# Four buffers in place of two for the inputs of a chunked scan, each loaded two tiles ahead

## The chip, the cores and the metric

The kernel runs on one core of one Trainium2 chip. The time is the device time of one execution in microseconds (us), and less is better. TensorE is called PE here, VectorE DVE, ScalarE ACT, GpSimd POOL and SyncE SP; SP computes nothing and issues most of the DMA transfers.

## What is computed

One layer of a diffusion backbone: a combined input projection, four mixers side by side, and an output projection. The change lies in the stage that runs two of the mixers together, neighbourhood attention (A) and gated linear attention (D). Cut to these two:

```python
# A: each query sees an 8x16 window of keys around it, and 512 context keys
s_lat = einsum('bhrqd,bhrikd->bhrqik', qg, kg) + bias
s_ctx = einsum('bhrqd,bhcd->bhrqc', qg, ck)
p = softmax(concatenate([s_lat, s_ctx], -1))
o = einsum('bhrqik,bhrikd->bhrqd', p_lat, vg) + einsum('bhrqc,bhcd->bhrqd', p_ctx, cv)

# D: a scan over chunks of 64 tokens, forward and backward
att = where(causal, einsum('bhntk,bhnsk->bhnts', q_dec, k_inv), 0)
o_intra = einsum('bhnts,bhnsv->bhntv', att, vc)
upd = einsum('bhnsk,bhnsv->bhnkv', k_end, vc)
def step(state, inp):
    d_c, u_c = inp
    return d_c[..., None] * state + u_c, state
o_inter = einsum('bhntk,bhnkv->bhntv', q_dec, s_start)
```

## The kernel before

The stages follow one another: modulation, two projection stages, this attention and scan stage, a Fourier stage, the output stage. Between stages all engines meet at a barrier.

The stage `attention_scan_stage` walks over 34 tiles of 128 tokens. A tile `i` of the grid is a block of 8 rows (`jb`, `b`) and one of four column strips (`c`, 0 to 3), so four tiles make a block; tiles 32 and 33 are the prompt. In the same step a tile does attention for its 128 queries, head by head (`h`, 0 to 3), and two chunks of the scan in each direction. Tiles 0 to 7 and 24 to 33 are written out, tiles 8 to 23 run in a loop over pairs of blocks.

Each engine has its own list of instructions, written by hand and tied together by semaphores. What matters here:

- **SP**, at the start of tile `i`, waits until PE is done with all of tile `i-1` (`pv_done`, `od_mm`). Then it issues, in this order: the values of tile `i+1` (`load_values`, four DMAs into `v_win`), the scan's inputs of tile `i+1` (`load_scan`, two DMAs into `scan` and two into `kv`), and one part of the next block's input: the queries at `c` = 0 (`q_hi`, `q_lo`), the keys' high part at `c` = 1 (`k_hi`), their low part at `c` = 2 (`k_lo`). After that it waits for the tile's output and stores it. All these DMAs go through one queue, SP's.
- **PE** does for each head `turn` (transposes of the probabilities, L1265 for the window and L1273 for the context), `scores` for later heads (L1244), and `values` (L1301). At `h` = 0 the last matmuls of `values` wait for the scan's inputs (`t_in`), after which `scan_scores` uses them (L1310). At `h` = 1 of the strip `c` = 3, the transposes of L1273 wait for the next block's keys (`k_in`), since the scores that follow need them.
- **POOL** reorders the queries of tile `i+1` (`order_queries`, L1118, semaphore `q_set`) and keeps the running state (`keep_state`, L1135, L1139). Ahead of the first tile it orders tile 0's queries, then waits for the initial state `s_at` (`st_in`); only then does it order tile 1's queries, for which PE waits at L1273 of tile 0, head 1.

Ahead of the tiles SP issues the masks' biases for the first strip, the values and the scan's inputs of tile 0, then `s_at`, then the other biases:

```python
            load_bias(0, BLOCKS - 1)
            load_values(0, BLOCKS - 1, 0)
            load_scan(0, 0)
            for d in DIRS:
                sp.dma_start(s_at[here(d), :]...).then_inc(st_in, 16)
```

Of the kernel before, what the change touches and what calls it, by code (L numbers as in the profile page):

```python
# [24 lines left out]
P = 128  # L25
# [8 lines left out]
W_GRP = 256  # L34
# [841 lines left out]
def attention_scan_stage(nc, io, keep, early):  # L876
# [15 lines left out]
    DIRS = range(2)  # L892
# [6 lines left out]
    with stage(nc) as (ctx, new_sem):  # L899
# [20 lines left out]
        max_c, max_w, neg_m, total, r_total = (sb(n, [P, 2]) for n in ("max_c", "max_w", "neg_m", "total", "r_total"))  # L920
        sums = sb("sums", [P, 2, 2])
        ones = sb("ones", [P, NH, P])
        scan = two("scan", [P, 3 * 512 + 8])
        kv = [two(f"kv{d}_", [P, 2, 2 * W_GRP]) for d in DIRS]
        mask = sb("mask", [P, C])
        s_at, s_mid, s_dec = (sb(n, [P, W_GRP]) for n in ("s_at", "s_mid", "s_dec"))
        od_sb = two("od_sb", [P, 2, W_GRP])
# [18 lines left out]
             "q_set", "s_done", "maxc_done", "w_done", "max_done", "exp_done", "sum_done", "rsum_done", "t_done", "t0_sb", "t1_sb", "pv_done", "o_done",  # L946
             "att_mm", "att_sb", "upd_mm", "mid_set", "mid_done", "new_set", "new_done", "kept", "od_mm", "od_done", "st_out"))
        bias_in = [sem(f"bias_in{e}") for e in range(3)]
        k_in, q_in, v_in, t_in, o_sent, od_sent = ([sem(f"{n}{s}") for s in range(2)] for n in ("k_in", "q_in", "v_in", "t_in", "o_sent", "od_sent"))
        block = ctx.enter_context(nc.Block())  # L950

        def tile_of(d, i):
# [31 lines left out]
        def _(sp):  # L984
# [44 lines left out]
            load_bias(0, BLOCKS - 1)  # L1029
            load_values(0, BLOCKS - 1, 0)  # L1030
            load_scan(0, 0)
            for d in DIRS:
                sp.dma_start(s_at[here(d), :].rearrange("k (h v) -> k h v", h=NH), io["state_gla"][0, 0, d].rearrange("h k v -> k h v")).then_inc(st_in, 16)
            for e in range(1, 3):
# [3 lines left out]
            for tile in query_tiles(sp):  # L1038
                i, jb, b, c, kb = tile
                nxt = next_tile(*tile)  # L1040
                if not isinstance(i, int):
                    ni, nb = nxt[0], nxt[2]
                    ahead(sp, 4 * i, 4 * i + 5, b * (BQ * W_GRP * 4), *((key_at(nb) + 4 * m) * (GRID_W * P1_W * 4) for m in range(4)),
                          *(n for d in DIRS for n in (tile_of(d, ni) * (HD * SCAN_W * 4), tile_of(d, ni) * (P * 2 * W_GRP * 4), tile_of(d, i - 1) * (P * W_GRP * 4))))
                    if c == 0:
                        ahead(sp, jb * 16, jb * 8, (b + 1) * (BQ * 4))
                    elif c < 3:
                        ahead(sp, key_at(b + 1) * (GRID_W * 4))
                if nxt:
                    if not isinstance(i, int) or i:  # L1050
                        sp.wait_ge(pv_done, 4 * i)
                        sp.wait_ge(od_mm, i)
                    load_values(nxt[0], nxt[2], nxt[3])
                    load_scan(nxt[0], nxt[3] % 2)
                if c < 3 and b is not None:
                    after = next_tile(i + 3 - c, jb, b, 3, kb)
                    if c == 0:
                        if not isinstance(jb, int) or jb:
                            sp.wait_ge(s_done, jb * 16)
                            sp.wait_ge(q_set, jb * 8)  # L1060
                        load_queries(after[1], after[2], after[4])
                    else:
                        load_keys(after[1], after[2], after[4], c - 1)
                if isinstance(jb, int) and jb < 2 and c in (0, 2, 3):
                    e = (0, None, 1, 2)[c]
                    sp.wait_ge(bias_clear, 3 + 3 * jb + e + 1)
                    load_bias(e, jb)
                sp.wait_ge(o_done, 4 * i + 5)
                if b is None:
                    sp.dma_start(io["ya"][i * P:(i + 1) * P, :], o_sb[c % 2][:, :]).then_inc(o_sent[c % 2], 16)  # L1070
                else:
                    sp.dma_start(io["ya"][bass.ds(b * BQ, BQ), :].rearrange("(r x) n -> r x n", x=GRID_W)[:, c * QB_C:(c + 1) * QB_C, :],
                                 o_sb[c % 2][:, :]).then_inc(o_sent[c % 2], 16)
                if not isinstance(i, int) or i:
                    sp.wait_ge(od_done, i)
                    for d in DIRS:
                        sp.dma_start(io["od"][d, bass.ds(tile_of(d, i - 1) * P, P), :], od_sb[1 - c % 2][:, d, :]).then_inc(od_sent[1 - c % 2], 16)
# [12 lines left out]
        def _(pool):  # L1090
# [33 lines left out]
            def keep_state(i, s, n):  # L1124
                state = s_mid if n else s_at
                if n:
                    pool.wait_ge(mid_done, i + 1)
                else:
                    pool.wait_ge(new_done, i + 1)
                    pool.wait_ge(t_in[s], (i - s) * 32 + 64)  # L1130
                    if not isinstance(i, int) or i > 1:
                        pool.wait_ge(od_mm, i - 1)
                for d in DIRS:
                    c = n if d == 0 else 1 - n
                    pool.tensor_tensor(kv[d][s][here(d), c, W_GRP:], state[here(d), :], ones[here(d), 0:2, :].rearrange("k a b -> k (a b)"), ALU.mult).then_inc(kept, 1)  # L1135
                pool.wait_ge(kept, 4 * i + 2 * n + 2)
                if not (n and isinstance(i, int) and i == GRID_T - 1):
                    heads = lambda a: a.rearrange("k (p h v) -> k p h v", p=2, h=2)
                    pool.tensor_tensor(heads(s_dec[:, :]), heads(state[:, :]), chunk_dec[s][:, :, :, n].unsqueeze(3).broadcast_to([P, 2, 2, HD]),  # L1139
                                       ALU.mult).then_inc(new_set if n else mid_set, 1)  # L1140
                else:
                    pool.sem_inc(new_set, 1)
# [4 lines left out]
            for tile in query_tiles(pool):  # L1147
                i, jb, b, c, kb = tile
                nxt = next_tile(*tile)
                if nxt:  # L1150
                    order_queries(*nxt)
                keep_state(i, c % 2, 0)
                if isinstance(jb, int) and jb < 2 and c in (0, 2, 3):
                    pool.wait_ge(max_done, 4 * i + 4)
                    e = (0, None, 1, 2)[c]
                    clear_bias(e)
                    pool.wait_ge(bias_clear, 3 + 3 * jb + e + 1)
                keep_state(i, c % 2, 1)

        @block.scalar  # L1160
        def _(act):
# [65 lines left out]
        def _(pe):  # L1227
# [48 lines left out]
            def values(tile, h):  # L1276
# [15 lines left out]
                for n, (m, val) in enumerate(todo):  # L1292
                    if n == len(todo) - 1:
                        if h == 0:
                            pe.wait_ge(t_in[s], (i - s) * 32 + 64)
                            if not isinstance(i, int) or i:
                                pe.wait_ge(od_done, i)
                        elif h == 1:
                            pe.wait_ge(att_sb, 2 * i + 2)
# [44 lines left out]
            for tile in query_tiles(pe):  # L1344
                i, jb, b, c, kb = tile
                for h in range(NH):
# [1 line left out]
                    scores(units_ahead(tile, h, 3), units_ahead(tile, h, 2))  # L1348
                    values(tile, h)
                    if h == 0:  # L1350
                        scan_scores(i, c % 2)
                    elif h == 1:
                        scan_updates(i, c % 2)
                    elif h == 3:
                        scan_out(i, c % 2)

        @block.vector
        def _(dve):
# [47 lines left out]
            for tile in query_tiles(dve):  # L1406
                i, jb, b, c, kb = tile
                for h in range(NH):
# [9 lines left out]
                    cols = N_PROMPT if b is None else WIN_P  # L1418
                    dve.tensor_copy(p_t[p][:, 0:cols], ps_t[0][:, 0:cols]).then_inc(t0_sb, 1)  # L1419
                    if h == 1:  # L1420
                        mask_scores(i, c % 2)
                    elif h == 2:
                        first_update(i)
                    elif h == 3:
# [448 lines left out]
```

## Time and profile before

| | us |
|---|---|
| median of 3 runs | 2808.14 (2800.19 to 2809.13) |
| the profiled execution | 2806.83 |
| its span, first to last instruction | 2805.1 |
| the stage's 34 tiles, from PE's first matmul of the stage to its last scan output | 1642.5 to 2223.7 |
| PE busy over the whole span | 2565.9 (91%) |
| PE busy from 1660 to 2224 | 527.7 of 564 |

The rows of the next section are of three kinds. In the **timeline** a row is a run of like instructions on one engine: start and length in us, engine, source line, what it writes and reads, the shape and how many; in brackets the time for which the engine stood idle before it, and what ended that. In the **waits** a row says which engine and line waited for what: us in total, how many times, the longest. In the **windows** a row is a stretch of time: its length, the busy time of PE, PE's weight loads, DVE, ACT and POOL with the number of instructions, the clock that PE was granted (1.00 is 2.4 GHz, 0.50 is 1.2 GHz), the mean busy share of the core's 16 DMA engines, and the GB/s that they moved. A share a little over 1 comes from packets that overlap on an engine. A row of the **DMA issues** gives how many, their size, and the median time from issue to landing, where it is known.

### The profile page before, as it was taken

How to read it: one execution, taken by the hardware profiler on the slowest of the kernel's cores; microseconds unless marked ns; L12 is line 12 of the kernel's file. 1: busy time of each engine (PE TensorE's matmuls, PEld its weight loads, DVE VectorE, ACT ScalarE, POOL GpSimd, SP SyncE). 2: the span in 40 equal slices, each digit the busy share in tenths (PEclk: the TensorE clock that was granted, in tenths of full speed). 3: DMA queues.
4: the chain of work that ended last, by engine and by line, in shares of the span. 5: the costliest groups of instructions: out<-in, count | busy, mean ns of one | idle time of the engine just before them, and what ended most of it. 6: DMA issues, size and time to landing. Idle time of an engine off the chain costs nothing. (4 is left out here: it accounts for less than half of the span.)

```text
span 2805.1 us, 53370 instructions
## 1 busy us (share of the span) xinstructions
PE 2565.9 (91%) x19036; PEld 2056.4 (73%) x19036; DVE 1271.6 (45%) x2644; ACT 984.1 (35%) x1991; POOL 740.7 (26%) x1145
## 2 busy tenths in 40 slices
PE   3899999999999949999999969998999764999999
PEld 1688888888888838888888857777777522788887
DVE  2444344344343343333333336776777322666555
ACT  2444444444444342222222125565656311111110
POOL 2233333233233210000000024333333201344442
PEclk8999999999999979999999979999999687999999
DMA  7433333333333263222222268877776497766664
GB/s 287 145 103 119 114 111 118 108 115 121 101 120 117 76 215 123 97 97 93 93 93 95 71 133 175 178 172 162 166 164 157 123 289 216 243 210 213 205 202 136
DMA packets 281020, 412.05 MB, mean 147 GB/s; under 512 B 43893, under 2 KB 201365, under 8 KB 277291
## 3 DMA queue, kind: packets, MB, share of 16 engines
q1 hardware_dynamic: 267372, 376.67, 46.6%
q10 hardware_dynamic: 12959, 32.33, 3.2%
q8 instruction: 95, 1.56, 0.3%
q0 software_dynamic: 544, 1.09, 0.2%
q14 instruction: 50, 0.41, 0.1%
HBM read 275.64 MB, written 134.34 MB: 146 GB/s over the span
## 5 line engine op out<-in xcount | busy, mean ns | idle before, releaser
L258 PE MATMUL p_ps_m<-p_w_hi,p_h_hi 128*128 128x512 f32 x1904 | 771.0, 405 | 21.1 <-DVE p_h_lo L779 19.4
L259 PE MATMUL p_ps_m<-p_w_lo,p_h_hi 128*128 128x512 f32 x1904 | 750.7, 394 | 0.0
L260 PE MATMUL p_ps_m<-p_w_hi,p_h_lo 128*128 128x512 f32 x1904 | 749.2, 393 | 0.0
L258 PEld LDWEIGHTS p_ps_m<-p_w_hi,p_h_hi 128*128 128x128 f32 x1904 | 359.3, 189 | 100.3 <-issue 20.2
L260 PEld LDWEIGHTS p_ps_m<-p_w_hi,p_h_lo 128*128 128x128 f32 x1904 | 358.8, 188 | 80.6
L259 PEld LDWEIGHTS p_ps_m<-p_w_lo,p_h_hi 128*128 128x128 f32 x1904 | 359.4, 189 | 72.6
L258 PE MATMUL o_ps_y<-o_w_hi,o_y_hi 128*128 128x512 f32 x544 | 217.4, 400 | 9.8 <-DVE o_y_lo L1773 9.8
L260 PE MATMUL o_ps_y<-o_w_hi,o_y_lo 128*128 128x512 f32 x544 | 217.4, 400 | 0.0
L259 PE MATMUL o_ps_y<-o_w_lo,o_y_hi 128*128 128x512 f32 x544 | 215.6, 396 | 0.0
L770 DVE TENSOR_TENSOR p_xt<-p_xt,p_ps_r 128x1024 f32<-128x1024 f32 x68 | 82.7, 1216 | 193.4 <-PE p_ps_r L679 193.4
L512 POOL TENSOR_TENSOR p_ve<-p_ss,p_eps 128x1 f32<-128x1 f32 x68 | 12.9, 190 | 565.5 <-ACT p_xr L576 565.5
L552 POOL TENSOR_TENSOR p_la<-p_la,p_cum 128x512 f32<-128x512 f32 x34 | 44.0, 1294 | 426.7 <-ACT p_cum L589 426.7
L773 DVE TENSOR_SCALAR p_xt<-p_xt,mod 128x128 f32<-128x128 f32 x544 | 146.1, 344 | 2.5
L1419 DVE COPY a_p_t<-a_ps_t 128x512 f32<-128x512 f32 (+1 forms) x136 | 91.7, 674 | 117.0 <-PE a_ps_t L1265 116.8
L779 DVE TENSOR_TENSOR p_h_lo<-p_xt,p_h_hi 128x1024 fp32r<-128x1024 f32 x68 | 83.3, 1226 | 98.8 <-ACT p_h_hi L581 98.8
L1699 ACT ACTIVATE o_y_hi<-o_ps_t 128x512 fp32r<-128x512 f32 x68 | 36.9, 596 | 258.4 <-PE o_ps_t L1728 258.4
L258 PEld LDWEIGHTS o_ps_y<-o_w_hi,o_y_hi 128*128 128x128 f32 x544 | 102.8, 189 | 33.3 <-issue 10.1
L259 PEld LDWEIGHTS o_ps_y<-o_w_lo,o_y_hi 128*128 128x128 f32 x544 | 102.8, 189 | 25.0
L260 PEld LDWEIGHTS o_ps_y<-o_w_hi,o_y_lo 128*128 128x128 f32 x544 | 102.7, 189 | 23.8
L1301 PEld LDWEIGHTS a_ps_o<-a_v_win,a_p_t 128*64 128x64 f32 x2112 | 75.9, 141 | 54.6 <-issue 39.2
L1370 DVE TENSOR_REDUCE a_max_c<-a_ps_c 128x1 f32<-128x512 f32 x128 | 88.1, 688 | 45.2 <-PE a_ps_c L1244 43.9
L1301 PE MATMUL a_ps_o<-a_cv,a_p_t 128*64 128x64 f32 x2048 | 91.0, 225 | 18.6 <-DMA a_kv<-s_kv 16.5
(216 smaller groups left out, 4541.3 us busy)
## 6 DMA issues: line engine op xcount, KB each, us to landing
p_xr<-in_x_sample SPq DMA_DIRECT2D x64, 512.0 KB, 3.8
p_xt<-in_x_sample_t SPq DMA_DIRECT2D x64, 512.0 KB, 4.5
a_scan<-s_scan SPq DMA_DIRECT2D x68, 258.0 KB, 5.9
s_scan<-p_w_raw SPq DMA_DIRECT2D x136, 128.0 KB, 2.4
a_kv<-s_kv SPq DMA_DIRECT2D x68, 256.0 KB, 6.2
a_v_win<-s_p SPq DMA_DIRECT2D x132, 128.0 KB
o_x<-in_x_sample SPq DMA_DIRECT2D x32, 512.0 KB, 4.5
out_y_sample<-o_y ACTq DMA_DIRECT2D x32, 512.0 KB, 4.4
```

The source lines that it names most:

```text
L258: pe.matmul(out, left_hi(k), right_hi(k), start=(k == 0), stop=False)
L259: pe.matmul(out, left_hi(k), right_lo(k), start=False, stop=False)
L260: last = pe.matmul(out, left_lo(k), right_hi(k), start=False, stop=(k == K8 - 1))
L512: pool.tensor_tensor(ve[s][:, :], ss[s][:, :], eps[:, 0:1], ALU.add).then_inc(ve_done, 1)
L552: pool.tensor_tensor(la[:, :, :], la[:, :, :], cum[:, :, :], ALU.subtract).then_inc(la_done, 1)
L770: dve.tensor_tensor(xt[s][:, :, :], xt[s][:, :, :], ps_r[:, s, :].unsqueeze(1).broadcast_to([P, K8, P]), ALU.mult).then_inc(normed, 1)
L773: last = dve.tensor_scalar(xt[s][:, k, :], xt[s][:, k, :], keep["mod"][:, 1, k, j:j + 1], keep["mod"][:, 0, k, j:j + 1], ALU.mult, ALU.add)
L779: dve.tensor_tensor(h_lo[s][:, :, :], xt[s][:, :, :], h_hi[s][:, :, :], ALU.subtract).then_inc(lo_done, 1)
L1301: last = pe.matmul(ps_o[z * HD:z * HD + HD, at:at + HD], p_t[p][:, m * P + z * HD:m * P + z * HD + HD], val, start=(n == 0), stop=(n == le ...
L1370: dve.tensor_reduce(max_c[:, p:p + 1], ps_c[p][:, :], AX.X, ALU.max).then_inc(maxc_done, 1)
L1419: dve.tensor_copy(p_t[p][:, 0:cols], ps_t[0][:, 0:cols]).then_inc(t0_sb, 1)
L1699: act.activation(y_hi[s][:, 4 * b:4 * b + 4, :], ps_t[b][:, :, :], ACT.Copy).then_inc(hi_done, 1)
```

## The change

Four buffers of `scan` and `kv` stand in place of two, one for each strip `c`, and four semaphores `t_in`. In tile `i` SP issues the scan's inputs of tile `i+2`, at the place where it issued those of `i+1`; ahead of the tiles it issues those of tile 0 and of tile 1. POOL, before it writes the state into `kv`, waits for the scan output of tile `i-4` in place of that of tile `i-2`. PE, DVE and ACT do the same work in the same order. Nothing else moves.

```diff
-        scan = two("scan", [P, 3 * 512 + 8])
-        kv = [two(f"kv{d}_", [P, 2, 2 * W_GRP]) for d in DIRS]
+        scan = [sb(f"scan{c}", [P, 3 * 512 + 8]) for c in range(4)]
+        kv = [[sb(f"kv{d}_{c}", [P, 2, 2 * W_GRP]) for c in range(4)] for d in DIRS]
...
+        t_in = [sem(f"t_in{c}") for c in range(4)]
...
             load_scan(0, 0)
+            load_scan(1, 1)
             for d in DIRS:
                 sp.dma_start(s_at[here(d), :]
...
                     load_values(nxt[0], nxt[2], nxt[3])
-                    load_scan(nxt[0], nxt[3] % 2)
+                    if not (isinstance(i, int) and i + 2 > LAST_STEP):
+                        load_scan(i + 2, (c + 2) % 4 if b is not None else c + 2)
...
-                    pool.wait_ge(t_in[s], (i - s) * 32 + 64)
-                    if not isinstance(i, int) or i > 1:
-                        pool.wait_ge(od_mm, i - 1)
+                    pool.wait_ge(t_in[s], (i - s) * 16 + 64)
+                    if not isinstance(i, int) or i > 3:
+                        pool.wait_ge(od_mm, i - 3)
...
-                            pe.wait_ge(t_in[s], (i - s) * 32 + 64)
+                            pe.wait_ge(t_in[c], (i - c) * 16 + 64)
```

Two places on SP show it. The first is ahead of the tiles: SP's rows from the values of tile 0 to the biases of the second and third strip, before (numbers behind a name are the buffers):

```order
L1007 DMA a_v_win0<-s_p1 128x1x256 x4
L1013 DMA a_scan0<-s_scan 64x1032
L1015 DMA a_kv0_0<-s_kv 64x2x512
L1013 DMA a_scan0<-s_scan 64x1032
L1015 DMA a_kv1_0<-s_kv 64x2x512
L1033 DMA a_s_at<-in_state_gla 64x4x64 x2
L1023 DMA a_bias<-s_btab 16x4x256 x16
```

And now, the same place on SP:

```order
L1008 DMA a_v_win0<-s_p1 128x1x256 x4
L1014 DMA a_scan0<-s_scan 64x1032
L1016 DMA a_kv0_0<-s_kv 64x2x512
L1014 DMA a_scan0<-s_scan 64x1032
L1016 DMA a_kv1_0<-s_kv 64x2x512
L1014 DMA a_scan1<-s_scan 64x1032
L1016 DMA a_kv0_1<-s_kv 64x2x512
L1014 DMA a_scan1<-s_scan 64x1032
L1016 DMA a_kv1_1<-s_kv 64x2x512
L1035 DMA a_s_at<-in_state_gla 64x4x64 x2
L1024 DMA a_bias<-s_btab 16x4x256 x16
```

Four more DMAs, the scan's inputs of tile 1, stand between those of tile 0 and the initial state. The second place is tile 2, the strip `c` = 2 of a block: SP's rows from the scan's inputs to the low part of the keys, before:

```order
L1013 DMA a_scan1<-s_scan 64x1032
L1015 DMA a_kv0_1<-s_kv 64x2x512
L1013 DMA a_scan1<-s_scan 64x1032
L1015 DMA a_kv1_1<-s_kv 64x2x512
L987 DMA a_k_lo1<-s_qk_lo 128x2x960
```

And now:

```order
L1008 DMA a_v_win1<-s_p1 128x1x256 x4
L1014 DMA a_scan0<-s_scan 64x1032
L1016 DMA a_kv0_0<-s_kv 64x2x512
L1014 DMA a_scan0<-s_scan 64x1032
L1016 DMA a_kv1_0<-s_kv 64x2x512
L988 DMA a_k_lo1<-s_qk_lo 128x2x960
```

The number of DMAs, their sizes and their place ahead of `k_lo` are the same; only the tile that they are for is another (tile 4 in place of tile 3).

## Rows read from the trace of the kernel before

**Rows 1.** Window of the stage, from tile 0's second head to the last tile.

```profile
1660.00:2224.00 564.00, 527.73 (x9160) 421.34 (x9159) 386.21 (x1039) 318.13 (x814) 203.48 (x333) 0.97 0.72 162
```

**Rows 2.** Waits of PE in the whole stage, from 1656 to 2226.

```profile
PE a_ps_o L1301 <- DMA a_kv<-s_kv: 16.5, 15, 2.7
```

**Rows 3.** Waits of PE in tiles 12 to 15 (1863 to 1930).

```profile
PE a_ps_o L1301 <- DMA a_kv<-s_kv: 3.3, 3, 1.3
```

**Rows 4.** Waits of PE in tiles 20 to 27 (1999 to 2134).

```profile
PE a_ps_o L1301 <- DMA a_kv<-s_kv: 5.0, 4, 1.8
PE a_ps_t L1273 <- DMA k_lo<-s_qk_lo: 1.0, 1, 1.0
...
PE a_ps_t L1273 <- DMA a_k_lo<-s_qk_lo: 0.6, 1, 0.6
```

**Rows 5.** Timeline of SP in tile 14, strip c = 2.

```profile
1897.33 4.70 SPq L1007 DMA_DIRECT2D a_v_win<-s_p  x4
...
1904.96 0.72 SPq L1015 DMA_DIRECT2D a_kv<-s_kv  x1
1905.78 0.55 SPq L987 DMA_DIRECT2D k_lo<-s_qk_lo  x1
```

**Rows 6.** Timeline of PE in tile 15, heads 0 and 1.

```profile
1916.38 0.34 PE L1301 MATMUL a_ps_o<-a_cv,a_p_t 128*64 128x64 f32 x4 [1.02 <-DMA a_kv<-s_kv]
...
1917.73 0.66 PE L1265 MATMUL a_ps_t<-ident,a_s_sb 128*128 128x128 f32 x4
1918.97 0.66 PE L1273 MATMUL a_ps_t<-ident,a_s_sb 128*128 128x128 f32 x4 [0.58 <-DMA k_lo<-s_qk_lo]
```

**Rows 7.** Windows in and just after tiles 12 to 15.

```profile
1867.00:1881.00 14.00, 13.99 (x240) 11.04 (x238) 10.55 (x27) 8.83 (x23) 4.07 (x8) 1.00 0.86 163
...
1899.00:1904.00 5.00, 4.39 (x82) 3.62 (x82) 2.46 (x6) 2.26 (x6) 2.07 (x3) 1.00 0.28 102
1904.00:1913.00 9.00, 8.99 (x166) 7.34 (x165) 7.24 (x22) 5.77 (x15) 3.75 (x7) 1.00 1.05 225
1916.00:1919.00 3.00, 2.04 (x41) 1.66 (x41) 0.76 (x3) 0.99 (x3) 2.07 (x3) 1.00 0.28 100
1933.00:1935.00 2.00, 1.69 (x14) 1.35 (x14) 1.02 (x3) 0.59 (x2) 0.78 (x2) 1.00 0.08 20
```

**Rows 8.** DMA issues of the stage.

```profile
a_scan<-s_scan SPq DMA_DIRECT2D x68, 258.0 KB, 5.9
a_kv<-s_kv SPq DMA_DIRECT2D x68, 256.0 KB, 6.2
a_v_win<-s_p SPq DMA_DIRECT2D x132, 128.0 KB
```

**Rows 9.** Timeline of SP ahead of the tiles.

```profile
1641.19 1.47 SPq L1013 DMA_DIRECT2D a_scan<-s_scan  x1
...
1644.03 0.61 SPq L1015 DMA_DIRECT2D a_kv<-s_kv  x1
1644.68 1.27 SPq L1033 DMA_DIRECT2D a_s_at<-in_state_gla  x2
```

**Rows 10.** Timeline of POOL at the start: the queries of tile 1.

```profile
1658.15 0.87 POOL L1118 TENSOR_TENSOR a_q_hi_t<-q_hi,a_ones 128x128 fp32r<-128x128 f32 x2 [15.94 <-DMA a_s_at<-in_state_gla]
1658.97 0.87 POOL L1118 TENSOR_TENSOR a_q_lo_t<-q_lo,a_ones 128x128 fp32r<-128x128 f32 x2
```

**Rows 11.** Timeline of PE in tile 0, heads 0 and 1.

```profile
1657.52 0.34 PE L1301 MATMUL a_ps_o<-a_cv,a_p_t 128*64 128x64 f32 x4 [2.70 <-DMA a_kv<-s_kv]
...
1659.02 1.11 PE L1265 MATMUL a_ps_t<-ident,a_s_sb 128*128 128x128 f32 x4
1659.99 1.09 PE L1273 MATMUL a_ps_t<-ident,a_s_sb 128*128 128x128 f32 x4
```

**Rows 12.** Windows at the start of the stage.

```profile
1643.00:1651.00 8.00, 5.54 (x22) 3.48 (x19) 3.60 (x11) 2.10 (x6) 0.00 (x0) 0.50 1.05 194
1651.00:1657.50 6.50, 3.82 (x37) 2.59 (x35) 1.89 (x7) 1.41 (x5) 0.00 (x0) 0.68 1.02 134
```

More of the change, by code:

```diff
@@ L948, in attention_scan_stage @@
         bias_in = [sem(f"bias_in{e}") for e in range(3)]
-        k_in, q_in, v_in, t_in, o_sent, od_sent = ([sem(f"{n}{s}") for s in range(2)] for n in ("k_in", "q_in", "v_in", "t_in", "o_sent", "od_sent"))
+        k_in, q_in, v_in, o_sent, od_sent = ([sem(f"{n}{s}") for s in range(2)] for n in ("k_in", "q_in", "v_in", "o_sent", "od_sent"))
+        t_in = [sem(f"t_in{c}") for c in range(4)]
         block = ctx.enter_context(nc.Block())
@@ L1041, in _ @@
                 if not isinstance(i, int):
-                    ni, nb = nxt[0], nxt[2]
+                    ni, nb = i + 2, nxt[2]
                     ahead(sp, 4 * i, 4 * i + 5, b * (BQ * W_GRP * 4), *((key_at(nb) + 4 * m) * (GRID_W * P1_W * 4) for m in range(4)),
@@ L1151, in _ @@
                     order_queries(*nxt)
-                keep_state(i, c % 2, 0)
+                keep_state(i, c, 0)
                 if isinstance(jb, int) and jb < 2 and c in (0, 2, 3):
@@ L1157, in _ @@
                     pool.wait_ge(bias_clear, 3 + 3 * jb + e + 1)
-                keep_state(i, c % 2, 1)
+                keep_state(i, c, 1)
         @block.scalar
@@ L1350, in _ @@
                     if h == 0:
-                        scan_scores(i, c % 2)
+                        scan_scores(i, c)
                     elif h == 1:
-                        scan_updates(i, c % 2)
+                        scan_updates(i, c)
                     elif h == 3:
-                        scan_out(i, c % 2)
+                        scan_out(i, c)
         @block.vector
@@ L1420, in _ @@
                     if h == 1:
-                        mask_scores(i, c % 2)
+                        mask_scores(i, c)
                     elif h == 2:
```

## The prediction

> **What bounds the kernel now.** I looked first at who waits for whom in the stage that the change touches. PE is the engine that sets its end: from 1660 to 2224 it is busy for 527.73 of 564 us, so some 36 us are open [rows 1]. About half of that, 16.5 us, are waits at L1301 for the last of the scan's inputs, `kv`, 15 times and 2.7 us at the longest [rows 2]. That is the wait that the change bears on, 0.6% of the span of 2805.1.
>
> Next I asked why these inputs are late. In tile 14 SP issues the last of tile 15's at 1904.96 [rows 5] and PE goes on at 1916.38 [rows 6]: 11.4 us. The median landing of such a DMA is 6.2 us [rows 8]. A view of the DMA engines by stretches explains the difference. In tiles 12 to 15 the mean share of the 16 engines goes to and fro between about 1.05 and 0.28 [rows 7]: all 16 are busy, then 0.28 x 16 = 4.5 of them go on alone, moving 100 GB/s, for 5 us and for 3 us. I read this as a few engines that carry more than the others. The one transfer that can do this is `v_win`: four DMAs of 128 KB for a tile [rows 8], with four rows of the window outermost. After k_lo has landed the share falls to 0.08 [rows 7], so there is idle time, but only once in a block. From 1867 to 1919, from the first values of the block to the landing of `k_lo`, I find no such gap: within a block these few engines work without rest, and what lands last is set by how much is queued on them, not by when it was asked for.
>
> Then I looked at what PE waits for just after `kv`. In tile 15 the wait for `kv` ends at 1916.38, and at L1273 of head 1, which starts at 1918.97, PE waits another 0.58 us, now for `k_lo` [rows 6], issued right behind the same `kv` at 1905.78 [rows 5]. The same wait ends the blocks of tiles 20 to 23 and 24 to 27, with 1.0 and 0.6 us [rows 4].
>
> **The change, part by part.**
>
> *The waits that go.* Tile 0's own inputs come no earlier, so its 2.70 us [rows 11] stay: 16.5 - 2.7 = 13.8 us in 14 waits are left to gain. With inputs issued a whole tile earlier, the wait for `kv` goes; a tile lasts some 16 us and they land in 11.4.
>
> *What is late next.* In tile 14 the same four transfers still stand ahead of `k_lo` on the same queue, with the same bytes; they are for tile 16 now. So `k_lo` lands when it did, counted from the block's first loads, and PE, which comes to L1273 earlier by all that it no longer waited for, waits there. In tiles 12 to 15 the gain of 3.3 us [rows 3] turns into 0.6 [rows 6] + 3.3 = 3.9 us of waiting for `k_lo`: nothing is gained. The same holds for the 5.0 us of tiles 20 to 27 [rows 4], which hold two such blocks. That leaves 13.8 - 3.3 - 5.0 = 5.5 us in the other blocks, where PE does not wait for `k_lo` before the change. There the gain is what `k_lo` has in hand. From below: 0, if it lands just as PE arrives, as in the three blocks shown. From above: all 5.5. The nearest rows are the three blocks in which nothing is in hand, so I take the lower part: 2.0 us gained.
>
> *Four more DMAs ahead of the tiles.* They are 2 x 258 + 2 x 256 KB = 1028 KB [rows 8], 1.05 million bytes, and go into SP's queue between tile 0's inputs and `s_at`, the initial state. `s_at` is on the path: POOL stands 15.94 us for it, then orders the queries of tile 1 until 1658.97 + 0.87 = 1659.84 [rows 10], and PE's L1273 of head 1, which needs them, starts at 1659.99, while the transposes before it run from 1659.02 for 1.11 us, so PE is not held up now but has at most 0.15 us in hand [rows 11]. Every microsecond by which `s_at` lands later is one for PE. From below: SP's own time for issuing four such DMAs, from 1641.19 to 1644.68 [rows 9], 3.5 us. From above: the bytes at the lower rate of this stretch, 134 GB/s, 7.9 us; at 194 GB/s it is 5.4 us [rows 12]. The DMA engines are full here (1.05 and 1.02), SP is ahead of them (`s_at` is issued at 1644.68 and lands by 1658.15, 13.5 us later), so it is the bytes that count and not the issuing. I take 5.4 us, since the bytes would go at the rate of the stretch in which tile 0's went. The Trainium skill (DMA: Bandwidth & Descriptors, Queues, rings and completion order) says that on each DMA engine descriptors are consumed in ring order; by that `s_at` queues behind the added bytes and the term is 5.4, and if it could pass them it would be the 3.5 of the issuing or less. The rows here cannot show the order on one engine.
>
> *Edits that cost nothing.* POOL's wait for tile `i-4` in place of `i-2` only gets weaker. In the tiles SP issues as many DMAs as before, at the same place and behind the same waits. The last two tiles load less, but their load was moved to the front. Two more semaphores and 28 KB more memory for a partition cost no instruction in the tiles. POOL's own waits for `kv` vanish too, but POOL waits for DVE behind them and nobody for it.
>
> **The sum.** The profiled execution took 2806.83, its span 2805.1. Less 2.0, plus 5.4: 2810.2. The median of the three runs is 2808.14, 1.3 above the profiled one, and from there it would be 2811.5. I say **2811 us**, with a range of its own of 2805 (2806.8 - 5.5 + 3.5) to 2815 (2806.8 + 7.9). A change of 0.3%, 8.4 us, is about what a measurement of this kernel can tell from none, so this is no change.
>
> **The rivals.**
>
> *A: the waits really go.* If `k_lo`, too, lands earlier, because the few slow engines have slack in the block that I did not see, or because PE's earlier arrival lets SP issue it earlier and that counts, all 13.8 us are gained. For it: in four of seven blocks PE does not wait for `k_lo`, and the DMA engines do rest after each block (0.08). Against it: the three blocks where `k_lo` follows within 3 us of `kv`. It gives 2806.8 - 13.8 + 5.4 = 2798.4. The Trainium skill (DMA: Bandwidth & Descriptors, Rules for kernel authors) advises to issue a DMA early and wait late; by that rule the waits are gone, as here. No row shows a `k_lo` that lands before PE wants it with microseconds to spare. Chance 0.15.
>
> *B: slower.* The start costs more than its bytes: 7.9 us at the low rate, and PE, which stands idle longer, comes back at the low clock. It had 0.50 from 1643 to 1651 and 0.68 on average from 1651 to 1657.5 [rows 12]; four transposes took 1.11 us in tile 0 against 0.66 in tile 15 [rows 11, 6], so six more microseconds of work at that pace cost 6 - 6 x 0.66 / 1.11 = 2.4 us. With nothing gained in any block that is 2806.8 + 7.9 + 2.4 = 2817. It decides where the wait for `s_at` grows by over 8.4 us with all that follows. Chance 0.08.
>
> *C: the start costs nothing.* `s_at`, which is small, may pass the added bytes on engines that have little to do, or POOL's lateness may be taken up behind. Then it is 2806.8 - 2.0 = 2805. Chance 0.15. Against it: 13.5 us for 128 KB of `s_at`, which did not pass anything.
>
> The main case keeps 0.62.
>
> **How the numbers follow.** The range of 2797 to 2817 holds the main case, C, the better part of A, and B up to its price. Faster by over 0.3% means below 2799.7: two thirds of A and a little of C, 0.12. Slower means above 2816.6: half of B and the upper end of the main case, should the start cost 7.9 and the clock as well, 0.10. The rest, 0.78, is within 0.3%.
>
> **What would show it right or wrong.** Right: in the waits, `kv` at L1301 falls from 15 waits and 16.5 us to one or two with about 3 us, and `k_lo` at L1273 grows from three waits and 2.2 us to seven with 10 us or more; in tile 15 L1273 starts as long after the block's first loads as before; POOL waits for `s_at` some 21 us in place of 15.94, and PE waits for POOL before L1273 of tile 0. Wrong: `k_lo` is not waited for longer than before, and the tiles 8 to 27 are shorter by some 10 us; or POOL gets `s_at` as early as now; or a wait for `v_win`, which I take to land in time because it stands first in the queue, takes the place of the one for `kv`.

## The result and the profile after

The changed kernel takes 2823.39 us (median of 7 runs, 2813.19 to 2828.65) against 2805.43 of the kernel before, run beside it: a ratio of 1.0064, with a 95% interval of 1.0046 to 1.0082. It is slower, where I had forecast no change (2811, at most 2817). The profiled execution has a span of 2824.2 us, 19.1 more than before. The kernel after has three more lines ahead of the stage's code: its L1304, L1276, L1313 and L1268 are L1301, L1273, L1310 and L1265 of before.

The whole loss lies in the attention and scan stage. From PE's first matmul of the stage to its last scan output it lasts 599.9 us (1641.1 to 2241.0) in place of 581.2. First the waits of PE in the stage after the change (1630 to 2250):

```profile
...
PE a_ps_g L1313 <- issue: 12.5, 5, 3.8
PE a_ps_t L1268 <- issue: 11.9, 4, 3.7
PE a_ps_t L1276 <- DMA k_lo<-s_qk_lo: 8.4, 2, 5.0
PE a_ps_t L1276 <- POOL a_q_lo_t L1121: 5.6, 1, 5.6
...
PE a_ps_o L1304 <- DMA a_kv<-s_kv: 1.4, 1, 1.4
...
PE a_ps_o L1304 <- DMA a_v_win<-s_p: 0.6, 1, 0.6
PE a_ps_t L1276 <- DMA a_k_lo<-s_qk_lo: 0.6, 1, 0.6
```

The waits for `kv` are gone but for tile 0's: 1.4 us in place of 16.5 [rows 2]. The waits for `k_lo` have grown from 2.2 us to 9.0 in three waits. And there is one that I had not thought of: L1313, the scan's scores, stands 12.5 us for "issue", for nothing that the profile shows. In the kernel before the same two lines read:

```profile
PE a_ps_t L1265 <- issue: 10.3, 4, 3.5
...
PE a_ps_g L1310 <- issue: 1.1, 2, 0.7
```

Next, tiles 4 to 27 as one window, from the end of tile 3's last scan output to the end of tile 27's. Before:

```profile
1724.70:2133.70 409.00, 381.63 (x6721) 304.40 (x6722) 285.63 (x768) 236.12 (x601) 144.75 (x243) 0.99 0.75 168
```

After:

```profile
1731.40:2151.90 420.50, 388.45 (x6723) 311.04 (x6722) 293.81 (x770) 237.00 (x601) 145.28 (x245) 0.96 0.73 163
```

These two rows are the heart of it. The work is the same (6721 and 6723 matmuls). The six blocks last 11.5 us longer. Of that, 32.05 - 27.37 = 4.7 us is more idle time, and 388.45 - 381.63 = 6.8 us is the same matmuls taking longer, at a mean granted clock of 0.96 in place of 0.99. The rest of the stage's 18.7 us lies at the start: tile 0 takes 35.6 us in place of 29.4, tiles 1 to 3 54.7 in place of 52.9 (from the end of one tile's last scan output to that of the next), while the last six tiles are 0.9 shorter.

Each block, divided at the landing of `k_lo`, shows where the time is lost. In the kernel before, PE starts its L1273 of the strip c = 3, head 1, within 0.3 us of that landing in all six of these blocks, also in those where the waits have no row for `k_lo`. In tile 11 `k_lo` is issued at 1839.71 and lands 12.5 us later, at 1852.18, and PE comes just then:

```profile
1851.58 0.66 PE L1265 MATMUL a_ps_t<-ident,a_s_sb 128*128 128x128 f32 x4
1852.23 0.66 PE L1273 MATMUL a_ps_t<-ident,a_s_sb 128*128 128x128 f32 x4
```

So the keys already set how long a block lasts, and no block had time in hand. Up to the landing the six blocks take 343.0 us before and 344.1 after; from the landing to the end of the block they take 66.1 before and 76.4 after. Some 10.3 of the 11.5 us are lost there. These are the two parts of the block of tiles 12 to 15, before:

```profile
1863.10:1918.92 55.82, 51.93 (x923) 41.45 (x922) 38.75 (x106) 32.99 (x84) 19.52 (x33) 1.00 0.74 171
1918.92:1929.84 10.92, 10.86 (x198) 8.58 (x198) 8.80 (x23) 6.60 (x17) 3.75 (x7) 1.00 0.60 146
```

And after:

```profile
1872.84:1927.55 54.71, 51.26 (x922) 41.34 (x922) 41.90 (x108) 33.34 (x84) 18.34 (x32) 1.00 0.76 173
1927.55:1939.96 12.41, 12.35 (x198) 9.58 (x198) 7.22 (x20) 6.50 (x17) 4.97 (x9) 0.86 0.56 130
```

Behind the landing the same 198 matmuls take 1.5 us longer, at a mean clock of 0.86. In the six blocks this clock is 1.00 before and 0.83 to 0.94 after.

Where the clock is lost shows in tile 15, the strip c = 3 that [rows 5 and 6] show before. First SP in tile 14, then PE in tile 15, after the change:

```profile
1905.92 4.80 SPq L1008 DMA_DIRECT2D a_v_win<-s_p  x4
...
1914.31 0.55 SPq L988 DMA_DIRECT2D k_lo<-s_qk_lo  x1
```

```profile
1923.48 0.65 PE L1268 MATMUL a_ps_t<-ident,a_s_sb 128*128 128x128 f32 x4
1927.60 1.11 PE L1276 MATMUL a_ps_t<-ident,a_s_sb 128*128 128x128 f32 x4 [3.46 <-DMA k_lo<-s_qk_lo]
1928.64 0.77 PE L1247 MATMUL a_ps_w<-k_hi,a_q_hi_t 64*128 64x480 f32 x1
```

`k_lo` is asked for 8.39 us after the values (1905.92 to 1914.31; before 8.45 [rows 5]) and lets PE go 13.3 us after that (before 13.2, [rows 5, 6]). So it lands when it did, and PE, which no longer stood for `kv` on the way, stands for it in one piece: 3.46 us in place of 1.02 and 0.58 [rows 6]. Then the four transposes take 1.11 us in place of 0.66. The windows around that wait:

```profile
1919.40:1924.20 4.80, 4.73 (x83) 3.75 (x82) 2.69 (x10) 3.29 (x9) 0.70 (x2) 1.00 0.95 214
1924.20:1927.60 3.40, 0.01 (x1) 0.01 (x1) 2.04 (x3) 0.00 (x0) 0.00 (x0) 1.00 0.26 98
1927.60:1931.00 3.40, 3.40 (x24) 2.35 (x26) 0.68 (x2) 1.27 (x3) 0.00 (x0) 0.50 0.58 163
1931.00:1934.00 3.00, 3.00 (x66) 2.70 (x64) 1.62 (x7) 1.14 (x4) 0.00 (x0) 1.00 1.07 201
```

PE works at 1.00 (2.4 GHz), stands for 3.4 us, works 3.4 us at 0.50 (1.2 GHz), and is back at 1.00. In the same place of the kernel before, behind its two short waits, the clock stayed at 1.00:

```profile
1919.00:1923.00 4.00, 4.00 (x78) 3.29 (x79) 3.20 (x9) 2.37 (x6) 0.00 (x0) 1.00 0.58 167
```

Tile 11, also a strip c = 3, shows the other new stall. PE's timeline and three windows, after the change:

```profile
1854.80 0.67 PE L1313 MATMUL a_ps_g<-a_scan 64*64 64x64 f32 x15
1859.33 1.22 PE L1313 MATMUL a_ps_g<-a_scan 64*64 64x64 f32 x17 [3.85 <-issue]
```

```profile
1851.20:1855.50 4.30, 3.70 (x63) 2.89 (x61) 2.66 (x9) 2.81 (x8) 0.70 (x2) 1.00 1.06 200
1855.50:1859.30 3.80, 0.00 (x0) 0.00 (x0) 0.00 (x0) 0.40 (x2) 0.00 (x0) 1.00 0.73 169
1859.30:1862.40 3.10, 3.07 (x25) 2.46 (x25) 0.74 (x2) 0.00 (x0) 0.00 (x0) 0.51 0.28 102
```

PE stops in the middle of a run of 32 equal matmuls, 15 done and 17 to come, so no semaphore can be what it waits for. The DMA queues tell what moves then, first in the full stretch (share 1.06) up to 1856.3, then in the stall:

```profile
q1 hardware_dynamic: 334, 0.97, 104.0%
```

```profile
q1 hardware_dynamic: 412, 0.63, 70.8%
q8 instruction: 1, 0.02, 2.4%
```

One packet of 16 KB from the queue named instruction is moved in the stall, from 1856.39 to 1857.84, and PE goes on 1.5 us after it. In tiles 3 and 7 it is the same: packets until 1717.85 and 1789.35, PE at 1719.36 and 1790.90. In tiles 19 and 27 it goes on 1.3 and 1.4 us after one. I read this as PE standing without instructions. It is read from the trace; no run here delays a fetch by itself. Why the packet comes no earlier stays open: the mean DMA share is 1.03 from 1853.00 to 1856.39, ahead of it, and still 0.99 from there to 1857.84, while it moves, so full engines alone do not keep it out.

In tiles 4 to 27 PE is granted 0.50 for 37.5 us in eight places after the change, and for 10.2 us in three before. Two of the eight go with the waits for `k_lo` (tiles 15 and 23), four with the stops at L1313 (tiles 7, 11, 19 and 27) and two with stops at L1268 (tiles 5 and 16).

Last, the start. POOL and PE after the change:

```profile
1662.11 0.86 POOL L1121 TENSOR_TENSOR a_q_hi_t<-q_hi,a_ones 128x128 fp32r<-128x128 f32 x2 [21.24 <-DMA a_s_at<-in_state_gla]
```

```profile
1657.21 1.11 PE L1268 MATMUL a_ps_t<-ident,a_s_sb 128*128 128x128 f32 x4
1663.93 1.09 PE L1276 MATMUL a_ps_t<-ident,a_s_sb 128*128 128x128 f32 x4 [5.61 <-POOL a_q_lo_t L1121]
```

POOL stands 21.24 us for `s_at` (15.94 before, [rows 10]), and PE 5.61 us for POOL, which it did not before [rows 11].

### The profile page after: what moved, and what is told of

It is laid out like the page before. It is cut to its first block and busy times, and to the rows that moved or that the text cites. A ratio compares the mean times of both kernels' runs of the same rounds, so it can differ in the third digit from the quotient of the medians.

```text
span 2824.2 us, 53376 instructions
## 1 busy us (share of the span) xinstructions
PE 2572.3 (91%) x19036; PEld 2064.0 (73%) x19036; DVE 1281.1 (45%) x2644; ACT 984.8 (35%) x1991; POOL 740.9 (26%) x1145
## 5 line engine op out<-in xcount | busy, mean ns | idle before, releaser
L1138 POOL TENSOR_TENSOR a_kv<-a_s_mid,a_ones 64x256 f32<-64x256 f32 x68 | 49.4, 726 | 310.9 <-DVE a_s_mid L1395 308.1
L1304 PEld LDWEIGHTS a_ps_o<-a_v_win,a_p_t 128*64 128x64 f32 x2112 | 77.7, 143 | 58.4 <-issue 43.8
```

What stands on the lines that cost most here:

```text
L1304: last = pe.matmul(ps_o[z * HD:z * HD + HD, at:at + HD], p_t[p][:, m * P + z * HD:m * P + z * HD + HD], val, start=(n == 0), stop=(n == le ...
```

## The experiments

The ratios are to the kernel before, run on the same chip, with 95% intervals. Three theories were on trial: that the start costs some 6 us of its own; that the order of keys and scan's inputs decides what PE waits for; and that all of it is late because a few DMA engines carry the values.

**Tile 1's inputs later.** They are issued behind the biases, the rest is the changed kernel.

```diff
             load_scan(0, 0)
-            load_scan(1, 1)
             for d in DIRS:
...
+            load_scan(1, 1)
```

> The changed kernel with one thing undone: ahead of the tiles the scan's inputs of tile 1 are issued behind the initial state and the biases, not ahead of the initial state. Theory: the added bytes ahead of the initial state cost PE 5.6 us of waiting for POOL at L1276 of tile 0 and about 1 us of low clock behind it; so POOL has the initial state at about 16 us after tile 1's query wait begins as before, PE's wait for POOL in tile 0 is under 0.5 us, and the time is 6 us under the changed kernel's, a ratio to the kernel before of 1.004. Rival: the start is only where PE meets a pace that the DMA engines set for the first blocks anyway; the wait moves to the end of blocks 0 to 2 and the ratio stays at 1.0064.

Measured: 2819.84 us, 1.0061 (1.0039 to 1.0083), no different from the change itself. PE's wait for POOL is gone and tile 0 takes 29.6 us, 6.0 less. But tiles 1 to 3 take 62.1, 7.4 more, with waits for the keys and the values and stops at L1313 and L1321. So the start's loss goes where I had put it and comes up again within the first block: the keys that PE waits for in tile 3 land 78.1 us after the stage's first matmul, against 79.1 with the change and 70.7 before. The theory of a cost of its own is refuted, as long as the block's own pace is limited by its DMAs.

**Keys ahead of the scan's inputs.** In c = 1 and 2 the changed kernel issues the next block's keys before the scan's inputs.

```diff
+                    if c in (1, 2) and b is not None:
+                        after = next_tile(i + 3 - c, jb, b, 3, kb)
+                        load_keys(after[1], after[2], after[4], c - 1)
                     if not (isinstance(i, int) and i + 2 > LAST_STEP):
                         load_scan(i + 2, (c + 2) % 4 if b is not None else c + 2)
...
-                    else:
-                        load_keys(after[1], after[2], after[4], c - 1)
```

> The changed kernel, but in strips c = 1 and c = 2 the next block's keys are issued ahead of the scan's inputs, which now have a tile in hand. Theory: what PE waits for at the end of a block is k_lo standing behind 1028 KB of scan inputs on the queue; ahead of them it lands some 5 us earlier, the waits at L1276 for k_lo (9.0 us in three blocks) fall to under 1 us, PE keeps its full clock in the strip c = 3, and with the stalls of L1313 that fall into the same stretch up to 35 us go (the excess of the seven strips c = 3 over 15.55 us): 2790 to 2805 us, ratio to the kernel before 0.995 to 1.000. If the stalls of L1313 are not tied to k_lo, they stay and the gain is 15 us, ratio 1.001. Rival: the DMA engines are simply full, and the wait goes over to the values or the scan's inputs: ratio 1.005 or more.

Measured: 2792.84 us, 0.9964 (0.9948 to 0.9981). No wait for the keys is left; the start still costs, as it should. The waits of PE (1656 to 2226):

```profile
...
PE a_ps_t L1277 <- POOL a_q_lo_t L1122: 5.5, 1, 5.5
PE a_ps_g L1314 <- issue: 3.7, 2, 2.8
```

The order decides, and with it the L1313 stalls (L1314 here) fall from 12.5 to 3.7 us.

**Both moves together.**

> Both of the edits of the two runs before: tile 1's scan inputs behind the biases, the keys ahead of the scan's inputs in the tiles. Theory: the gains add, 6 us and 15 to 35 us under the changed kernel: 2783 to 2802 us, ratio to the kernel before 0.993 to 0.999. Rival (DMA engines full): ratio 1.003 or more.

Measured: 2789.1 us, 0.9948 (0.9927 to 0.9968). Faster than either kernel, though its interval overlaps that of the keys' move alone.

**The keys' move with two buffers.** The kernel before, with the same three lines.

> The kernel before with the one edit that made the changed kernel faster, and without the four buffers: in strips c = 1 and c = 2 the keys are issued ahead of the scan's inputs. Theory: with inputs only one tile ahead the 960 KB of keys ahead of them make kv land 3 to 4 us later in 14 tiles; the waits at L1301 grow from 16.5 to 50 us or more, and PE falls to its low clock behind the longer ones: ratio 1.010 to 1.020. Rival: the order of keys and inputs is what matters and the buffers do not; then the ratio is 0.995 to 1.000, as it was with four buffers.

Measured: 2810.57 us, 1.0023 (1.0009 to 1.0038). The sign was right, the size was not: I expected 50 us of waits for `kv` and there are 20.0.

```profile
PE a_ps_o L1302 <- DMA a_kv<-s_kv: 20.0, 12, 3.6
```

Against 0.9964 with four buffers, it shows what the buffers are for: room to let the keys go first.

**Four buffers, one tile ahead.** The changed kernel with the distance undone.

```diff
-            load_scan(1, 1)
...
-                    ni, nb = i + 2, nxt[2]
+                    ni, nb = nxt[0], nxt[2]
...
-                    if not (isinstance(i, int) and i + 2 > LAST_STEP):
-                        load_scan(i + 2, (c + 2) % 4 if b is not None else c + 2)
+                    load_scan(nxt[0], nxt[3])
```

> The changed kernel with the distance undone and the buffers kept: four buffers and four semaphores, but each tile issues the inputs of the next one, and ahead of the tiles only those of tile 0 are issued. Theory: buffers alone do nothing, since nothing waited for a free one: waits for kv at L1301 of 15 to 18 us as in the kernel before, no wait over 1.5 us for k_lo, ratio 0.998 to 1.002. Rival: something in the layout or the code of the changed kernel (more memory, other addresses, other code length) costs time by itself, above all at L1313, where PE now waits for nothing that is shown: ratio 1.004 or more and L1313 waits of 10 us.

Measured: 2805.97 us, 1.0007 (0.9994 to 1.002), and the waits of before:

```profile
PE a_ps_o L1302 <- DMA a_kv<-s_kv: 19.7, 16, 3.3
```

So the memory, the semaphores and the buffers' places cost nothing; the loss is the distance.

**Half of the values left out, after and before.** From tile 2 on only two of `v_win`'s four DMAs are issued; the work on them stays.

```diff
-                for m in range(4):
+                for m in range(4 if isinstance(i, int) and i < 2 else 2):
...
```

> The changed kernel, but from tile 2 on only two of the four DMAs of the window's values are issued (half of that load is left out; the matmuls use what lies in the buffer). Theory: the values run on a few of the 16 DMA engines, and these carry k_lo's last part too; 256 KB less on them in a tile lets k_lo land some 8 us earlier in a block, so the waits for k_lo go, the low share of 0.28 in the windows lasts half as long, and the time falls by 15 to 35 us under the changed kernel's, ratio 0.995 to 1.001. Rival: it is the total of bytes that counts, of which 256 KB in about 2700 KB of a tile is a tenth; then k_lo lands 1 to 2 us earlier in a block and the gain is under 8 us, ratio 1.004 or more.

> The kernel before (two buffers, one tile ahead), but from tile 2 on only two of the four DMAs of the window's values are issued; half of that load is left out. Theory: kv is late in the kernel before because the values keep a few of the 16 engines busy ahead of it; with half of them gone, kv lands some 2.7 us earlier in a tile, more than the longest wait for it but tile 0's, so the waits at L1301 fall from 16.5 us to about 3 and the time by 16 to 22 us: ratio to the kernel before 0.992 to 0.995. Rival, the total of bytes counts: kv lands 1 us earlier, the waits fall to about half, ratio 0.997 or more.

Measured: 0.9928 (0.9901 to 0.9956) after, 0.9909 (0.9888 to 0.9929) before, in both a larger gain than I expected. With the changed kernel no wait for the keys and no stall at L1313 is left; with the kernel before the only wait for `kv` is tile 0's, 2.4 us. Two tiles ahead or one, the waits go when the values weigh half. This does not yet say whether their bytes count or the few engines that carry them.

**The values on all engines.** The kernel with both moves, each tile's values as 16 DMAs of one window row (32 columns) each.

```diff
-                for m in range(4):
+                for r in range(16):
...
-                    sp.dma_start(v_win[s][:, m, :], ...).then_inc(v_in[s], 16)
+                    sp.dma_start(v_win[s][r % 4 * WIN_KC:r % 4 * WIN_KC + WIN_KC, r // 4, :], ...).then_inc(v_in[s], 16)
...
```

> The kernel of four buffers with keys ahead and tile 1's inputs late (ratio 0.9948 above), and the same values of a tile in 16 DMAs of one window row (32 columns) each, in place of 4 DMAs of four rows. Theory: a DMA whose outermost dimension is 4 runs on 4 engines, one of 32 on all 16; the stretches with a share of 0.28 vanish, the values land some 4 us sooner, and the stage runs as in the run with half of the values or better: ratio 0.988 to 0.993. Against it stands SP's time: 16 issues at 0.53 us are 8.5 us, with the others some 14 of a tile's 15.5; if SP takes more, it sets the pace and the ratio is over 1.000.

Measured: 2797.65 us, 0.9975 (0.9963 to 0.9987): a miss, no faster than without it (0.9948, with an interval that just overlaps). PE now waits for the values:

```profile
PE a_ps_o L1304 <- DMA a_v_win<-s_p: 18.1, 13, 3.9
```

And SP, which stands 178.8 us of the stage for the tile's output in the kernel before and 139.7 in the kernel with both moves, stands 18.5. Its waits in this run:

```profile
...
SPq L1075 <- ACT a_o_sb L1198: 18.5, 8, 9.2
```

At 0.5 to 0.6 us for each DMA, I read SP's own issuing as the new pace. Nor do the stretches with a low share vanish, as I had expected: in slices of 0.25 us, the share lies between 0.18 and 0.36 for 58 us of tiles 4 to 27, against 120 with both moves alone.

**Half of the values on all engines.** The kernel with both moves; two of the four DMAs stay, two become eight of one row.

```diff
-                for m in range(4):
+                for m in range(2):
...
+                for r in range(8, 16):
...
+                    src = io["p1"][(key_at(b) + r) * GRID_W:(key_at(b) + r + 1) * GRID_W, P1_V:P1_G]
+                    sp.dma_start(v_win[s][r % 4 * WIN_KC:r % 4 * WIN_KC + WIN_KC, r // 4, :],
+                                 src[COL_BASE[c]:COL_BASE[c] + WIN_KC, :]).then_inc(v_in[s], 16)
...
```

> This is the kernel with both moves (the keys ahead of the scan's inputs, tile 1's inputs behind the biases), and half of each tile's values asked for in another shape: two of the four DMAs stay as they are, with four rows outermost, and the other two become eight DMAs of one row of 32 columns, which can be spread over all engines. The bytes are the same. Theory (the few engines that carry the values set the pace of a block, and SP has room for some 6 more DMAs a tile but not for 12): stretches with a share near 0.28 become shorter by half, no wait for the keys comes back, waits for the scan's inputs fall below 5 us, no long wait for the values comes up, and the ratio is 0.988 to 0.993, below the 0.9948 of the two moves alone. Rival (SP's issuing sets the pace as soon as there are more DMAs): waits for the values of over 8 us in the stage and a ratio of 0.995 or more. Second rival (the long gaps come from the number of packets, not from the few engines): ratio within 0.002 of 0.9948 and the share pattern unchanged.

Measured: 2770.58 us, 0.9877 (0.9855 to 0.9899), a little better than expected, with no wait of PE for keys, scan's inputs or values left, and 52 us with a share between 0.18 and 0.36 in place of 120. The same edit alone, on the kernel before and on the changed one:

> This is the kernel before (two buffers, inputs one tile ahead) with nothing changed but the shape of half the values' DMAs: two of the four stay, the other two become eight of one row of 32 columns. The bytes are the same. Theory (what is late is late because a few engines carry the values; the distance of the scan's inputs hardly matters): waits for the scan's inputs fall from 16.5 us to under 6, no wait for the keys comes up, ratio 0.989 to 0.994. Rival (the inputs need two tiles' time in any case): waits for the scan's inputs stay above 10 us and the ratio is 0.996 or more.

> This is the changed kernel (four buffers, two tiles ahead, keys behind the scan's inputs, tile 1's inputs ahead of the initial state) with nothing changed but the shape of half the values' DMAs, as in the other run. Theory: the long wait for the keys at c = 3 goes (under 1 us in all), since the few engines are no longer the pace of the block; PE's wait for POOL in tile 0 stays at 5 us or more; ratio 0.988 to 0.993, within 0.003 of the other run, so two tiles ahead is then worth nothing that can be told apart. Rival (the order of keys and scan's inputs decides, whatever the engines carry): waits for the keys of over 4 us in the stage, ratio 0.996 or more.

Measured: 2765.95 us, 0.9876 (0.9855 to 0.9897) with two buffers, and 2770.23 us, 0.9892 (0.9871 to 0.9912) with the change. With two buffers tiles 4 to 27 take 382.6 us in place of 409.0, with 6.6 us idle in place of 27.4:

```profile
1718.80:2101.40 382.60, 375.99 (x6721) 302.43 (x6722) 285.12 (x768) 237.50 (x601) 144.70 (x243) 0.99 0.66 179
```

In that run the scan's scores stop for 1.5 us in all, and the only wait of PE in the stage for one of its inputs is this:

```profile
PE a_ps_o L1309 <- DMA a_kv<-s_kv: 0.2, 1, 0.2
```

The low share is down to 54 us, from 121 in the kernel before. The keys land 47.7 to 55.4 us after a block's start, where it was 55.7 to 60.8, and PE comes to the transposes that need them 0.8 to 3.6 us later: they no longer set how long a block lasts. With the change PE's wait for POOL in tile 0 stays, but at 2.1 us, where I had expected 5 or more:

```profile
PE a_ps_t L1284 <- POOL a_q_lo_t L1129: 2.1, 1, 2.1
```

The bytes are all there, so it was the few engines that carried them, and not the volume, that made keys and inputs late. And once that is mended, one tile ahead with two buffers does as well as two ahead with four.

**PE kept busy while it waits.** In the changed kernel, at c = 3, head 1, the four transposes are done five times over before the wait for the keys.

```diff
+                    if h == 1 and tile[3] == 3 and local[0] and local[0][2] is not None:
+                        for _ in range(5):
+                            for m in range(CC):
+                                pe.transpose(ps_t[1][:, m * P:(m + 1) * P], ...)
...
```

> This is the changed kernel with idle PE time filled: in the strip c = 3, head 1, where PE would stand and wait for the low part of the keys, it first does the four transposes of L1276 five times over (about 2.7 us of work whose result is overwritten by the right one). The wait itself ends when the keys land, so nothing comes earlier. Theory (the long wait costs more than its length, since PE works at half clock for some 3 us after it): in tiles 15 and 23, where the wait is one for the keys, the 3 us behind the wait show a granted clock near 1.00 in place of 0.50, and the tiles' periods fall by 1 to 2 us, from 20.55 and 22.49. In the strips that stop at L1313 nothing is filled, so tiles 7, 11, 19 and 27 stay as they are or are up to 2.7 us longer where the keys have landed before PE comes. Total: ratio to the kernel before between 1.003 and 1.008 (1.0064 without the filling). Rival (the clock after the wait is not the price of the wait, only a companion): the low clock stays behind the wait, or goes and the periods of tiles 15 and 23 stay within 0.5 us; ratio 1.006 or more.

Measured: 2827.08 us, 1.009 (1.0064 to 1.0117). PE in tile 15:

```profile
1932.06 2.35 PE L1279 MATMUL a_ps_t<-ident,a_s_sb 128*128 128x128 f32 x20
1934.86 0.66 PE L1282 MATMUL a_ps_t<-ident,a_s_sb 128*128 128x128 f32 x4 [0.45 <-DMA k_lo<-s_qk_lo]
```

And the window behind that wait:

```profile
1934.80:1938.20 3.40, 3.34 (x68) 2.70 (x70) 1.61 (x6) 1.71 (x5) 0.00 (x0) 1.00 0.58 166
```

The transposes take 0.66 us and not 1.11, the clock stays at 1.00, and the tiles' periods fall from 20.55 to 18.23 us (tile 15) and from 22.49 to 17.57 (tile 23). Behind the landing of the keys this block, from 12.41 us, is back at the length that it has in the kernel before:

```profile
1934.82:1945.73 10.91, 10.86 (x198) 8.58 (x198) 7.23 (x20) 6.61 (x17) 4.96 (x9) 1.00 0.63 145
```

The blocks of tiles 20 to 23 and 24 to 27 take 11.0 and 11.2 us there, in place of 12.8 and 12.7. So the low clock comes from PE's standing still, and it costs 1.5 to 1.9 us in each of these three blocks. But the whole kernel is no faster, against what I expected: the block of tiles 12 to 15 takes 67.0 us against 67.1, since PE now stops 1.55 us for "issue" in tile 13, and in the stage its three largest groups of such stops come to 25.0 us, against 26.0 in the changed kernel. The other three blocks are 1.0 to 2.1 us longer. In those of tiles 4 to 7 and 16 to 19 the keys have landed 5.2 and 2.4 us before PE is done with the extra work; in tile 11 a wait of 2.25 us for the keys is left behind it, and PE is granted 0.50 again. What the low clock is worth in the total is not settled by this run. The 6.8 us of longer PE time, above, is what the rows give.

## Why the prediction was wrong

**What bounds the stage: right.** A few engines carry the values and what lands last is set by what is queued on them. The kernel before with nothing changed but the shape of half the values' DMAs bears it out (0.9876). The Trainium skill (DMA: Bandwidth & Descriptors, Rules for kernel authors) says that an outermost dimension of fewer than 16 confines a DMA to at most that many engines. The trace is close to that: four rows outermost, and 0.28 x 16 = 4.5 engines busy on average [rows 7].

**What is late next: right.** `k_lo` lands where it did: in all six blocks of tiles 4 to 27 it lands within 1.4 us of its time before, counted from the block's start. Rival A (the waits really go) is wrong, though the waits for `kv` did go. The rule of the Trainium skill that stood beside it (DMA: Bandwidth & Descriptors, Rules for kernel authors), to issue a DMA early and wait late, holds for the stream that was moved, but not for the time: the waits for `kv` fall from 16.5 to 1.4 us, but `k_lo` stands behind as many bytes of the same queue as before, and the time comes out 0.6% longer.

**The step that failed is the gain of 2.0 us in the blocks.** I took a wait that changes its name to cost the same, "nothing is gained", and so bounded the term at 0 from below. And I took the blocks in which PE does not wait for `k_lo` to have something in hand, 5.5 us at most. They had next to nothing: PE came to the keys within 0.3 us of their landing in all six blocks of tiles 4 to 27, and within 0.6 us in tile 3. So the gain had to be close to 0. It is a loss of 11.5 us in tiles 4 to 27, 10.3 of it behind the keys' landing. What I left out is what a long stop does to the work behind it. The short waits, spread over tiles with the clock mostly at 1.00 between them, became one stop in a block, ahead of or at the wait for the keys: 3.5 and 5.0 us for `k_lo` in tiles 15 and 23, and 1.9 to 3.9 us at L1313 in tiles 7, 11, 19 and 27. Behind it PE works 3 us and more at 0.50; the same matmuls take 6.8 us longer. The stops at L1313, 12.5 us in place of 1.1, I had not seen at all; that PE lacks instructions there is read, not shown. Where they come, the keys have landed or are about to when PE gets to its wait, so the row for `k_lo` shows three waits and 9.0 us in place of my seven with 10 or more. The idle time of the six blocks grows by 4.7 us.

**The term of the start: right in size, wrong as a term.** I took 5.4 us from the bytes; `s_at` is waited for 21.24 - 15.94 = 5.3 us longer and PE waits 5.61. Tile 0 is 6.2 us longer. But moving these DMAs away moves the loss into tiles 1 to 3 and the total stays (1.0061): the added bytes delay whatever stands behind them. Rival C is wrong at POOL.

**Rival B had the sign and half of the mechanism**, PE coming back at the low clock, but put it at the start alone. In the terms of the rows: 7.9 at the start and 2.4 for the clock were forecast, while tiles 0 to 3 lose 8.1 and the blocks behind them 11.5, which no rival had.

**The edits called free** were free: four buffers with the old distance give 1.0007.

## What to carry to other kernels

When PE waits for a stream in the same queue as others, loading it earlier only passes the wait on to the stream behind it: ask what lands last in the block and which engines carry it, and mend that first. No row in the waits does not mean time in hand: look how long before its use a transfer lands. Here it was the outermost dimension of one load, and reshaping half of it gave 0.9876 with two buffers and no new order. Price a wait by how it is cut: several short ones between which PE works can be cheaper than one that adds up to the same, since PE may come back from a long one at half its clock, here for 1.5 to 1.9 us a block.

## What the runs showed of the hardware

- After stops of 3.46 us (tile 15) and 3.85 us (tile 11) PE was granted 0.50 for the next 3 us or so; after stops of 1.02 and 0.58 us it kept 1.00. With 2.35 us of filling work and a stop of 0.45 us it kept 1.00 as well. The length of the one stop does not decide it alone: in the kernel before, PE fell to 0.50 some 1.6 us behind a wait of 1.76 us for `kv`, and kept 1.00 behind a stop of 3.47 us (rows below).
- A run of equal matmuls stopped for up to 3.85 us with no semaphore, until 1.3 to 1.6 us after a 16 KB packet of the instruction queue had been moved. With the values reshaped these stops at the scan's scores come to 1.1 us in place of 12.5 with the change, to 1.5 in place of 1.1 with two buffers, and to 6.6 in place of 6.4 with both moves. What decides where they come is not shown.
- Spreading a load over more engines has a price on the issuing side: with 16 DMAs in place of 4 for a tile's values, the time in which SP stands free for a tile's output fell from 139.7 to 18.5 us, and PE waited 18.1 us for the values. With half of them spread no such wait was left.

The rows of the first point, from the kernel before: how the two stops end, and the clock behind each.

```profile
1933.31 0.63 PE L1265 MATMUL a_ps_t<-ident,a_s_sb 128*128 128x128 f32 x4 [3.47 <-issue]
...
2035.89 0.34 PE L1301 MATMUL a_ps_o<-a_cv,a_p_t 128*64 128x64 f32 x4 [1.76 <-DMA a_kv<-s_kv]
```

```profile
1933.40:1936.80 3.40, 3.20 (x48) 2.39 (x49) 2.08 (x5) 1.76 (x4) 0.46 (x1) 1.00 0.16 35
2037.51:2040.92 3.41, 3.41 (x22) 2.36 (x22) 2.39 (x4) 1.27 (x3) 0.62 (x1) 0.50 0.46 136
```
